# Layer 0 of a hybrid decoder step: the next step's distances issued one by one between this step's masked copies

## The chip, the core and the metric

The kernel runs on one core of a Trainium2 chip. The metric is the device time of one launch in microseconds. A core has five engines with an instruction queue each, worked off in order: TensorE (PE in the profile, its weight loads PEld), VectorE (DVE), ScalarE (ACT), GpSimd (POOL) and SyncE (SP), which issues most DMAs here. They wait for each other through semaphores: an instruction raises a counter when it is done, and another engine, or the same one, waits until the counter has reached a value.

## The reference

One inference step of a two-layer trunk, float32. Layer 0 mixes tokens by gated linear attention (GLA), layer 1 by a Mamba-2 state space scan; both have RMS norms before and after, and a gate. There are 16 meta tokens, a prompt of 1024 tokens and 8 samples of one token each. The part that the change touches is the attention inside a chunk:

```
bcum   = cumsum(log_alpha)                                   # per head channel k, falling
decay  = exp(where(i >= j, bcum[i] - bcum[j], -inf))
attn   = einsum('bihk,bjhk,bijhk->bhij', q, k, decay)
o      = attn @ v + (q * exp(bcum)) @ S
S      = exp(b_last) * S + (k * exp(b_last - bcum))^T @ v
```

The decay depends on i, j and the channel k at once, so it can't be taken out of the product as one factor.

## The kernel before

**Tiling.** All products are made in full float32 precision from pairs of rounded parts, a high one (ScalarE makes it by a copy) and a low one (VectorE subtracts the high one from the full value): high by high, high by low, low by high. The columns (8 samples, 16 meta tokens, 1024 prompt tokens) are cut into nine steps: step 0 has 24 columns, steps 1 to 8 have 128 each. They form two groups, steps 0 to 4 and 5 to 8. For each layer, group and head unit u (four units) the input projections are run tile by tile (`Pieces`), and stored in DRAM. One unit behind, the recurrent part takes the stored columns step by step. A pair (u, s) is an event e; there are 36 in each layer.

**Order.** `Plan.skeleton` writes one list of tasks, and every engine walks this list and issues its own share of each task (`program`). For layer 0 the list of a step e is `gla`; a number beside a name shifts the event, ("decay", 1) is the decay of event e+1, ("turn", -1) the turn of event e-1. "fill" puts in pieces of the projections. In this order, in the stretch that matters: distance(e+1), keys(e), levels(e), decay(e+1), turn(e-1), fill, load(e+2), fill, state(e), fill, attend(e), scale(e+1), products(e-1).

**The attention of an event.** The triangle i >= j of 128 by 128 is cut into levels: blocks of 64, 32, ..., 1, and the diagonal. In a level with blocks of h, all pairs (i, j) of a block of 2h meet at its middle, and decay = exp(bcum[i] - mid) * exp(mid - bcum[j]).
- `dve_distance` (L1707 to L1726, VectorE) writes, for each of 7 levels, bcum minus its middle into one of the eight parts of the buffer E (`g_decays`, double by e % 2): L1723. The eighth part is bcum minus its last column, for the state: L1725. This last instruction alone raises the semaphore `dsub`.
- `act_decay` (ScalarE) makes exp(bcum) (L1737), waits for `dsub`, and takes absolute value (L1739) and exp (L1741) of all eight parts at once, 128 x 1024 elements each.
- `dve_scale` (VectorE) multiplies all parts by q (L1750) and by k (L1753).
- `pe_levels` (TensorE) makes the products of each level into two banks of PSUM, L1836 and L1839, levels 0 to 3 in the first half, 4 to 6 in the second, and the plain product of q and k for the diagonal last, L1842. The semaphore `levels` rises after each half.
- `dve_levels` (VectorE) picks from each bank, through a mask, the blocks of a level, and puts them into one matrix `g_attn`: six copies L1857 (levels 0 and 1 share one), and the diagonal L1861. All write the same matrix, so each waits for the one before by the semaphore `attn_part`.
- `pe_attend` (TensorE, L1933) multiplies `g_attn` with the values, `dve_gate` (L1940) gates the result, `pe_turn` (L1959) transposes it. `act_turn` (ScalarE, L1968) copies its high part to `g_ot_hi`, `dve_turn` (VectorE, L1976) makes the low part `g_ot_lo`, and `pe_products` (TensorE, helper line L790) multiplies with the output weights; before it, TensorE waits for `g_ot_lo`.

On ScalarE a step's queue is so: keys (L1811), decay of the next event (L1737, L1739, L1741), turn of the event before (L1968), then roundings of weights (L805), of `h` (L1387), and evictions of projection pieces. On VectorE: the eight distances of e+1, keys (step 0 only), the copies of e, `g_ot_lo` of e-1, work for pieces, state (L1926), gate (L1940), scaling of e+1.

Of the kernel before, what the change touches and what calls it, by code (L numbers as in the profile page):

```python
# [9 lines left out]
ALU = mybir.AluOpType  # L10
ACT = mybir.ActivationFunctionType

P = 128
D = 1024
KT = D // P
NS = 8
# [33 lines left out]
EVENTS = [(u, s) for G in range(2) for u in range(U) for s in GROUP_STEPS[G]]  # L50
# [5 lines left out]
def step_cols(s):  # L56

    return (0, C0) if s == 0 else (C0 + P * (s - 1), P)
# [6 lines left out]
def ev(u, s):  # L65

    return 5 * u + s if s < 5 else 5 * U + 4 * u + s - 5
# [7 lines left out]
def gla_levels(s):  # L75

    return ([8, 4, 2, 1], NS) if s == 0 else ([64, 32, 16, 8, 4, 2, 1], 0)


def gla_masks(s):  # L80

    return [0, 1, 2, 3] if s == 0 else [0, 2, 3, 4, 5, 6]
# [29 lines left out]
class Plan:  # L112
# [72 lines left out]
    def skeleton(self):  # L185
# [3 lines left out]
        def stage(L, name, e, first_only=False):  # L189
            if 0 <= e < len(EVENTS):  # L190
# [12 lines left out]
                else:  # L203
                    tasks.append((name, L, u, s))

        gla = [("distance", 1), ("keys", 0), ("levels", 0), ("decay", 1), ("turn", -1), ("fill", 0.5), ("load", 2),
               ("fill", 0.5), ("samples", 0.4), ("state", 0), ("fill", 0.5), ("attend", 0), ("scale", 1),
               ("products", -1), ("weight", 0, 0), ("values", 1), ("square", 0), ("r_add", -2), ("r_in", -1),
               ("fill", 0.5), ("lows",), ("fill", 0.5), ("weight", 1, 0), ("r_square", -1), ("r_out", -2),
# [1350 lines left out]
class Gla:  # L1560
# [143 lines left out]

    def dve_distance(self, dve, u, s):  # L1707
        t, e, n = self.t, ev(u, s), step_cols(s)[1]
        if e == 0:
            dve.wait_ge(self.zeros, 4)  # L1710
            dve.wait_ge(self.consts, self.CONSTS)
        x, E = self.tokens(u, s), t["E"][:, e % 2, :, :]
        sizes, off = gla_levels(s)
        dve.wait_ge(self.ck_in[e % 2], 16 * (e // 2 + 1))
        if e >= 2:
            dve.wait_ge(self.levels, 2 * (e - 1))
            dve.wait_ge(self.tb_done, e - 1)
        b = x[:, 2, off:n]
        if s == 0:
            dve.memset(E[:, :, 0:NS], 0.0).then_inc(self.zeros, 1)  # L1720
        for li, h in enumerate(sizes):
            v = b.rearrange("p (b w) -> p b w", w=2 * h)
            dve.tensor_tensor(E[:, li, off:n].rearrange("p (b w) -> p b w", w=2 * h), v,  # L1723
                              v[:, :, h - 1:h].to_broadcast([P, v.shape[1], 2 * h]), ALU.subtract)
        dve.tensor_tensor(E[:, 7, off:n], b, x[:, 2, n - 1:n].to_broadcast([P, n - off]),  # L1725
                          ALU.subtract).then_inc(self.dsub, 1)  # L1726

    def act_decay(self, act, u, s):
        t, e, n = self.t, ev(u, s), step_cols(s)[1]
# [113 lines left out]
            last.then_inc(self.levels, 1)  # L1843

    def dve_levels(self, dve, u, s):
        t, e, n = self.t, ev(u, s), step_cols(s)[1]
        g, mk = (t["G0"], t["mask0"]) if s == 0 else (t["G"], t["mask"])
        masks = gla_masks(s)
        if e:
            dve.wait_ge(self.o_done, e)  # L1850
        part = sum(len(gla_masks(q)) for _, q in EVENTS[:e])
        for i, li in enumerate(masks):
            if li % 4 == 0:
                dve.wait_ge(self.levels, 2 * e + li // 4 + 1)
            if i:
                dve.wait_ge(self.attn_part, part + i)
            dve.copy_predicated(g[:, :], mk[:, li, :].bitcast(I32),  # L1857
                                self.L[li // 4][0:n, (li % 4) * P:(li % 4) * P + n]).then_inc(self.attn_part, 1)
        dve.wait_ge(self.attn_part, part + len(masks))
        dve.wait_ge(self.levels, 2 * e + 2)  # L1860
        dve.copy_predicated(g[:, :], self.m["ident"][0:n, 0:n].bitcast(I32),  # L1861
                            self.L[1][0:n, 3 * P:3 * P + n]).then_inc(self.attn, 1)

# [728 lines left out]
```

## Time and profile before

| | |
|---|---|
| median of 3 runs | 1641.74 us (1635.92 to 1644.21) |
| the profiled execution | 1636.64 us, its span 1634.9 us |
| TensorE busy | 1518.6 us (93%) |
| VectorE busy | 1186.8 us (73%) |
| ScalarE busy | 824.5 us (50%) |
| GpSimd busy | 238.6 us (15%) |
| masked copies L1857, 192 of 128x128 | 57.9 us, 301 ns each |
| distances L1723, 224 of 128x128 | 47.8 us, 282 ns each |
| mean granted TensorE clock | 0.972 of full |

Busy time of an engine is the union of its instructions. Idle time of an engine that is not the bottleneck costs nothing by itself; it counts where the engine that is nearly always busy waits for it. A line of the profile names the engine, the source line, the operation, and "written tile <- read tiles". The recurrent part of layer 0 runs from about 85 to 740 us of the span. In a timeline, "idle before <- releaser" stands in brackets where an engine stood idle.

### The profile page before, as it was taken

The numbers are of one execution on the slowest core, as the hardware profiler recorded it, in microseconds if no ns is written. First come the engines' busy times: TensorE is split into PE (matmuls) and PEld (weight loads), VectorE is DVE, ScalarE is ACT, GpSimd is POOL, SyncE is SP. The second block draws the span as 40 slices with busy tenths as digits, with TensorE's granted clock in tenths as the row PEclk, the third lists the DMA queues.
The fourth block names the chain that finished last, engine by engine and source line by source line (L and its number), as shares of the span: only waits on it lengthen the run. The fifth ranks groups of instructions, "written<-read, shape, count | busy, mean of one in ns | idle before, by whom it ended". The sixth has DMA issues, their size and how long they took to land. (4 is left out here: it accounts for less than half of the span.)

```text
span 1634.9 us, 26150 instructions
## 1 busy us (share of the span) xinstructions
PE 1518.6 (93%) x8970; PEld 1266.4 (77%) x8970; DVE 1186.8 (73%) x2587; ACT 824.5 (50%) x1835; POOL 238.6 (15%) x427
## 2 busy tenths in 40 slices
PE   6989999899999979898999999889989999999876
PEld 5979777667878869898888888767777778778654
DVE  4556477957786887868887798876769676587665
ACT  4634343445455545546664664544546364554441
POOL 5010112001220200112110220210002110000002
PEclk8999999999999999999999999999999999999998
DMA  6454454344565533448855765743675765556641
GB/s 172 135 156 117 133 148 144 106 138 141 150 156 174 149 114 100 130 111 204 230 141 127 228 167 129 216 121 83 190 189 139 180 166 138 163 142 158 149 142 58
DMA packets 312095, 242.60 MB, mean 148 GB/s; under 512 B 32760, under 2 KB 283452, under 8 KB 311804
## 3 DMA queue, kind: packets, MB, share of 16 engines
q1 hardware_dynamic: 302140, 208.28, 47.3%
q0 software_dynamic: 9824, 32.64, 7.3%
q8 instruction: 73, 1.20, 0.3%
q14 instruction: 58, 0.48, 0.1%
HBM read 180.40 MB, written 64.97 MB: 150 GB/s over the span
## 5 line engine op out<-in xcount | busy, mean ns | idle before, releaser
L1377 PE MATMUL bank<-h,w 128*128 128x268 f32 (+1 forms) x4752 | 840.8, 331 | 32.7 <-ACT w L805 28.0
L1377 PEld LDWEIGHTS bank<-h,w 128*128 128x128 f32 x4752 | 704.4, 192 | 110.6 <-issue 41.2
L790 PE MATMUL bank<-s_w_out,s_yt_hi 128*128 128x512 f32 (+1 forms) x576 | 186.6, 405 | 15.7 <-DVE s_w_out L821 6.9
L819 DVE TENSOR_TENSOR w<-w_raw,w 128x1024 fp32r<-128x1024 f32 x132 | 160.9, 1219 | 52.5 <-ACT w L805 52.1
L805 ACT ACTIVATE w<-w_raw 128x1024 fp32r<-128x1024 f32 x132 | 138.7, 1051 | 37.7 <-DMA w_raw<-in_ssd_w_in_dram 37.2
L790 PEld LDWEIGHTS bank<-s_w_out,s_yt_hi 128*128 128x128 f32 (+1 forms) x576 | 103.0, 183 | 46.5 <-issue 8.9
L1455 DVE SCALAR_TENSOR_TENSOR conv<-before_conv,cw,conv 128x260 f32<-128x260 f32 (+2 forms) x216 | 125.2, 580 | 4.3
L790 PE MATMUL bank<-s_w_out,s_yt_lo 128*128 128x512 f32 (+1 forms) x288 | 115.3, 400 | 0.0
L790 PE MATMUL bank<-g_w_out,g_ot_hi 128*128 128x512 f32 (+1 forms) x288 | 100.5, 431 | 0.0
L2210 ACT ACTIVATE s_decay<-s_decay,t_ac 128x128 f32<-128x128 f32 (+1 forms) x288 | 85.4, 379 | 1.2
L1857 DVE COPY_PREDICATED g_attn<-g_lmask,bank 128x128 f32<-128x128 int32 (+1 forms) x208 | 60.6, 291 | 33.8 <-PE bank L1839 25.7
L1423 ACT ACTIVATE conv<-bank,cw 128x268 f32<-128x268 f32 (+1 forms) x72 | 45.9, 637 | 74.3 <-PE bank L1377 61.5
L2384 PEld LDWEIGHTS bank<-s_xdt,s_decay 128*128 128x128 f32 (+1 forms) x576 | 66.5, 183 | 19.3 <-issue 19.3
L1699 POOL TENSOR_SCALAR g_omean<-g_osum 128x1 f32<-128x1 f32 (+1 forms) x36 | 16.5, 459 | 431.0 <-ACT squares L1951 431.0
L2185 POOL TENSOR_SCALAR s_ymean<-s_ysum 128x1 f32<-128x1 f32 (+1 forms) x36 | 18.8, 521 | 399.5 <-ACT squares L2486 399.3
L2505 ACT ACTIVATE s_yt_hi<-bank 128x512 fp32r<-128x512 f32 (+1 forms) x36 | 20.0, 556 | 112.2 <-PE bank L2496 112.1
L2168 POOL DMA_DIRECT2D out_dram<-s_sample_state x32 | 25.1, 784 | 331.2 <-DVE s_sample_state L2322 331.2
L1527 DVE SCALAR_TENSOR_TENSOR stage<-stage,conv 128x268 f32<-128x268 f32 (+1 forms) x72 | 37.3, 518 | 49.2 <-ACT stage L1484 48.7
L1789 ACT ACTIVATE g_vr_turned<-bank 128x512 f32<-128x512 f32 (+1 forms) x36 | 21.3, 591 | 91.0 <-PE bank L1777 91.0
L790 PEld LDWEIGHTS bank<-g_w_out,g_ot_hi 128*128 128x128 f32 (+1 forms) x288 | 53.5, 188 | 17.4 <-issue 2.9
L2023 DVE SCALAR_TENSOR_TENSOR y_acc<-bank,s_yrstd,y_acc 128x512 f32<-128x512 f32 (+1 forms) x54 | 39.7, 745 | 35.5 <-PE bank L790 35.5
L2384 PE MATMUL bank<-s_xdt,s_decay 128*128 128x64 f32 (+1 forms) x576 | 65.3, 266 | 0.0
(230 smaller groups left out, 2513.8 us busy)
## 6 DMA issues: line engine op xcount, KB each, us to landing
w_raw<-in_ssd_w_in_dram SPq DMA_DIRECT2D x80, 512.0 KB, 4.2
w_raw<-in_gla_w_in_dram SPq DMA_DIRECT2D x48, 512.0 KB, 4.2
s_decay<-kept_acd SPq DMA_DIRECT2D x32, 512.0 KB, 8.4
w_raw<-in_ssd_w_out_dram SPq DMA_DIRECT2D x32, 512.0 KB, 4.3
g_chunk<-kept_gq SPq DMA_DIRECT2D x32, 448.0 KB, 5.0
s_chunk<-kept_sq SPq DMA_DIRECT2D x32, 384.0 KB, 4.9
kept_sq<-stage SPq DMA_DIRECT2D x80, 134.0 KB, 4.2
kept_sq<-stage SPq DMA_DIRECT2D x40, 256.0 KB, 4.6
```

Of the source, the lines that this page charges most:

```text
L790: last = pe.matmul(bank[0:n, :], yt[a][:, k, 0:n], wo[:, k, b, 512 * half:512 * half + 512], start=(k + a + b == 0), stop=(k == tiles - 1 ...
L805: act.activation(self.part(i, 0), self.raw(i), ACT.Copy).then_inc(self.w_hi, 1)
L819: dve.tensor_tensor(self.part(i, 1), self.raw(i), hi, ALU.subtract).then_inc(self.w_lo, 1)
L1377: last = pe.matmul(bank[:, 0:n], w[:, p.tile % 2, a, k, :], h[:, b, k, c:c + n], start=(i == 0), stop=(i == len(terms) - 1))
L1423: act.activation(self.work(i)[:, 0:n], bank[:, 0:n], ACT.Identity, scale=m["cw"][:, 3, a:a + 1], bias=m["cw"][:, 4, a:a + 1])
L1455: return dve.scalar_tensor_tensor(out=u[:, off:n], in0=x[:, k:k + w], scalar=cw[:, k, a:a + 1], in1=u[:, off:n], op0=ALU.mult, op1=ALU.add)
L1527: dve.scalar_tensor_tensor(out=self.slot(i)[:, 0:n], in0=self.slot(i)[:, 0:n], scalar=1.0, in1=self.work(i)[:, 0:n], op0=ALU.add, op1=ALU. ...
L1857: dve.copy_predicated(g[:, :], mk[:, li, :].bitcast(I32), self.L[li // 4][0:n, (li % 4) * P:(li % 4) * P + n]).then_inc(self.attn_part, 1)
L2023: return dve.scalar_tensor_tensor(out=y, in0=bank, scalar=rstd, in1=y, op0=ALU.mult, op1=ALU.add)
L2168: pool.dma_start(self.heads(self.d["ssm_sample"][0, b], u), self.t["ss"][:, i % SAMPLES, :, :]).then_inc(self.ss_out[i % SAMPLES], 16)
L2210: last = act.activation(L[0:n, r, :], L[0:n, r, :], ACT.Relu, scale=-1.0, bias=ac[0:n, s, h:h + 1])
L2384: last = pe.matmul(self.Y[0][0:n, r * HD:(r + 1) * HD], G[0:n, r, :], t["xdt"][0:n, r * HD:(r + 1) * HD], start=True, stop=True)
```

## The change

The task "distance" is taken out of the list `gla`, so that in the loop over events no distances are issued ahead of the copies. (The one for event 0, in the list `start`, stays.) `dve_levels` of event e now issues the distances of event e+1 itself: what they wait for and the first one ahead of the first masked copy, then one behind each masked copy, and the rest behind the diagonal copy. In an event of 128 columns that is: distance 0, six times copy and distance, diagonal copy, distance 7, the one that raises `dsub`. In an event of 24 columns it is distance 0, four times copy and distance, diagonal copy, and the remaining three. The arithmetic, the number of instructions, the buffers and the other engines' programs are the same.

```diff
-        gla = [("distance", 1), ("keys", 0), ("levels", 0), ("decay", 1), ("turn", -1), ("fill", 0.5), ("load", 2),
+        gla = [("keys", 0), ("levels", 0), ("decay", 1), ("turn", -1), ("fill", 0.5), ("load", 2),
...
+    def distance_ready(self, dve, u, s):
+        e = ev(u, s)
         if e == 0:
             dve.wait_ge(self.zeros, 4)
             dve.wait_ge(self.consts, self.CONSTS)
...
+    def distance(self, dve, u, s, li):
+
+        t, e, n = self.t, ev(u, s), step_cols(s)[1]
+        sizes, off = gla_levels(s)
+        b, E = self.tokens(u, s)[:, 2, off:n], t["E"][:, e % 2, li, off:n]
+        if li == 7:
+            dve.tensor_tensor(E, b, b[:, n - off - 1:n - off].to_broadcast([P, n - off]),
+                              ALU.subtract).then_inc(self.dsub, 1)
+        elif li < len(sizes):
+            h = sizes[li]
+            v = b.rearrange("p (b w) -> p b w", w=2 * h)
+            dve.tensor_tensor(E.rearrange("p (b w) -> p b w", w=2 * h), v,
+                              v[:, :, h - 1:h].to_broadcast([P, v.shape[1], 2 * h]), ALU.subtract)
...
     def dve_levels(self, dve, u, s):
...
+        following = EVENTS[e + 1] if e + 1 < len(EVENTS) else None
+        if following:
+            self.distance_ready(dve, *following)
+            if following[1] == 0:
+                dve.memset(t["E"][:, (e + 1) % 2, :, 0:NS], 0.0).then_inc(self.zeros, 1)
+            self.distance(dve, *following, 0)
         if e:
             dve.wait_ge(self.o_done, e)
...
             dve.copy_predicated(g[:, :], mk[:, li, :].bitcast(I32),
                                 self.L[li // 4][0:n, (li % 4) * P:(li % 4) * P + n]).then_inc(self.attn_part, 1)
+            if following:
+                self.distance(dve, *following, i + 1)
         dve.wait_ge(self.attn_part, part + len(masks))
         dve.wait_ge(self.levels, 2 * e + 2)
         dve.copy_predicated(g[:, :], self.m["ident"][0:n, 0:n].bitcast(I32),
                             self.L[1][0:n, 3 * P:3 * P + n]).then_inc(self.attn, 1)
+        if following:
+            for li in range(len(masks) + 1, 8):
+                self.distance(dve, *following, li)
```

## Rows read from the trace of the kernel before

**Rows 1.** Busy by stretch, layer 0: PE, PEld, DVE, ACT, POOL; clock, DMA, GB/s.
```profile
85.00:740.00 655.00, 624.42 (x3829) 521.32 (x3830) 471.02 (x1105) 310.80 (x617) 95.86 (x160) 0.98 0.48 135
```

**Rows 2.** Waits, 85 to 740 us: who <- for whom: us, times, longest.
```profile
ACT g_decays L1739 <- DVE g_decays L1725: 46.6, 25, 3.7
...
DVE g_attn L1857 <- PE bank L1839: 25.7, 12, 5.6
...
PE bank L1377 <- ACT w L805: 8.9, 3, 4.7
...
PE bank L1933 <- DVE g_attn L1861: 7.1, 3, 3.9
PE bank L1016 <- DVE h L1435: 6.8, 3, 3.1
```

**Rows 3.** Timeline of VectorE, one step: start, us, engine, line, operation.
```profile
573.68 1.50 DVE L1723 TENSOR_TENSOR g_decays<-g_chunk 128x128 f32<-128x128 f32 x7
575.10 0.28 DVE L1725 TENSOR_TENSOR g_decays<-g_chunk 128x128 f32<-128x128 f32 x1
575.30 2.04 DVE L1857 COPY_PREDICATED g_attn<-g_lmask,bank 128x128 f32<-128x128 int32 x6
577.38 0.30 DVE L1861 COPY_PREDICATED g_attn<-ident,bank 128x128 f32<-128x128 int32 x1
577.87 0.42 DVE L1976 TENSOR_TENSOR g_ot_lo<-bank,g_ot_hi 128x256 fp32r<-128x256 f32 x1 [0.18 <-ACT g_ot_hi L1968]
```

**Rows 4.** Timeline of ScalarE, the same step.
```profile
575.41 1.06 ACT L1739 ACTIVATE g_decays<-g_decays 128x1024 f32<-128x1024 f32 x1 [2.54 <-DVE g_decays L1725]
576.50 1.06 ACT L1741 ACTIVATE g_decays<-g_decays 128x1024 f32<-128x1024 f32 x1
577.47 0.37 ACT L1968 ACTIVATE g_ot_hi<-bank 128x256 fp32r<-128x256 f32 x1
```

**Rows 5.** Timeline of TensorE, the same step.
```profile
577.82 0.62 PE L1933 MATMUL bank<-g_vr_turned,g_attn 128*128 128x256 f32 x2
578.35 0.73 PE L790 MATMUL bank<-g_w_out,g_ot_hi 128*128 128x512 f32 x2
```

**Rows 6.** Timeline of VectorE, a copy followed by an instruction that isn't held.
```profile
444.60 0.30 DVE L1861 COPY_PREDICATED g_attn<-ident,bank 128x128 f32<-128x128 int32 x1
444.81 0.42 DVE L1976 TENSOR_TENSOR g_ot_lo<-bank,g_ot_hi 128x256 fp32r<-128x256 f32 x1
```

**Rows 7.** Timeline of VectorE, four other steps.
```profile
298.93 1.48 DVE L1723 TENSOR_TENSOR g_decays<-g_chunk 128x128 f32<-128x128 f32 x7
...
303.11 0.42 DVE L1976 TENSOR_TENSOR g_ot_lo<-bank,g_ot_hi 128x256 fp32r<-128x256 f32 x1 [0.19 <-ACT g_ot_hi L1968]
...
460.29 0.42 DVE L1976 TENSOR_TENSOR g_ot_lo<-bank,g_ot_hi 128x256 fp32r<-128x256 f32 x1 [0.19 <-ACT g_ot_hi L1968]
...
565.82 0.42 DVE L1976 TENSOR_TENSOR g_ot_lo<-bank,g_ot_hi 128x256 fp32r<-128x256 f32 x1 [0.19 <-ACT g_ot_hi L1968]
...
591.07 0.42 DVE L1976 TENSOR_TENSOR g_ot_lo<-bank,g_ot_hi 128x256 fp32r<-128x256 f32 x1 [0.20 <-ACT g_ot_hi L1968]
```

**Rows 8.** Timeline of TensorE, these four steps and one wait for weights.
```profile
300.61 0.39 PE L1842 MATMUL bank<-g_chunk 128*128 128x128 f32 x2
...
303.58 0.72 PE L790 MATMUL bank<-g_w_out,g_ot_hi 128*128 128x512 f32 x2
...
463.84 0.81 PE L790 MATMUL bank<-g_w_out,g_ot_hi 128*128 128x512 f32 x2
...
566.99 0.81 PE L790 MATMUL bank<-g_w_out,g_ot_hi 128*128 128x512 f32 x2
...
591.59 1.42 PE L790 MATMUL bank<-g_w_out,g_ot_hi 128*128 128x512 f32 x2
...
675.70 4.36 PE L1377 MATMUL bank<-h,w 128*128 128x268 f32 x18 [4.70 <-ACT w L805]
```

**Rows 9.** Timeline of ScalarE, the rounding of weights behind that wait.
```profile
674.51 1.05 ACT L805 ACTIVATE w<-w_raw 128x1024 fp32r<-128x1024 f32 x1
```

## What the change should do to the time

> **What bounds the kernel now.** I read the busy times first, of the stretch that the edit touches (layer 0, 85 to 740 us of the span): of its 655 us TensorE is busy for 624.4, VectorE for 471.0, ScalarE for 310.8 [rows 1]. A change on VectorE can only show where TensorE stands still, 30.6 us now, or will. Next came the waits of that window [rows 2]. TensorE waits there for the last masked copy (L1933, 7.1 us in 3 waits), for the `h` tile that a norm piece needs (L1016, 6.8 us in 3) and for weights rounded by ScalarE (L1377, 8.9 us in 3). The longest wait that the change is bound to touch is on neither engine: ScalarE waits 46.6 us, in 25 of 36 steps, for the last distance, before the absolute value in `act_decay` (L1739). And VectorE waits 25.7 us, in 12 steps, for the level products on TensorE (L1857). These 12 are steps in which VectorE comes early; in the others it comes late, with everything else ready.
>
> Then one late step in order of time, engine by engine [rows 3 to 5]. VectorE does seven distances from 573.68, the last (L1725) until 575.38, six masked copies from 575.30, the diagonal copy until 577.68, then waits 0.18 us for `g_ot_hi` and splits off `g_ot_lo` until 578.29. ScalarE starts Abs at 575.41, 0.03 us after the last distance, Exp at 576.50 and the copy to `g_ot_hi` at 577.47, one right behind the other. TensorE starts `attend` (L1933) at 577.82 and the output products (L790) at 578.35, 0.06 us after `g_ot_lo`. So two chains end at about the same point of TensorE's queue: copies -> attend, and last distance -> Abs -> Exp -> `g_ot_hi` -> `g_ot_lo` -> products. The second is 0.5 us the later one, and it is the one that hangs on the distances.
>
> **The change, part by part.** No instruction and no DMA goes or comes; what moves is the order on VectorE. In a full step (128 columns, followed by another such) there are 8 distances and 7 copies.
>
> Spacing. Distances start 0.20 us apart ((575.30-573.68)/8), though each is 0.28 long: they overlap. Copies that wait for one another start 0.347 apart ((577.38-575.30)/6) [rows 3]. An instruction that isn't held starts 0.20 us after a copy has started: 444.60 to 444.81 [rows 6]. So I take copy, distance 0.20 later, next copy 0.20 after that, at 0.404, when its predecessor's signal (0.347) is already there. From the start of the step: 0.20 for distance 0, six pairs of 0.404, diagonal copy from 2.63 to 2.93, last distance from 2.83 to 3.11. Before: diagonal copy ended at 4.00, last distance at 1.70. Hence the attention matrix is ready 1.07 us earlier, VectorE is through 0.89 us earlier, and the last distance comes 1.41 us later.
> Bounds for the last distance: if the distances vanish wholly behind the held copies (pair 0.347), it ends at 2.76, +1.06. If nothing overlaps (pair 0.347+0.202), at 3.97, +2.27, with attention only 0.2 earlier. No bound reaches zero, because the last distance stands behind six chained copies in any case. I take +1.41, since rows 6 show the overlap directly.
> The Trainium skill ("VectorE: DVE Perf Modes", section "The DRAIN you can't avoid") says that a signal between chained operations costs nothing and that the flush is paid either way. By it the upper bound would hold: +2.27, and some 31 us in all. The 0.347 against 0.20 above speaks against it here.
>
> Abs, Exp and `g_ot_hi` stand in ScalarE's queue in this order, before and after, and all pass the +1.41 on: in rows 4 there is no idle time between them. Behind `g_ot_lo` in VectorE's queue are the state update, the gate and the next scaling, so VectorE as well comes out 1.4 us later; the 0.89 us that it saved is spent idle, waiting for `g_ot_hi`. Ahead of the products in TensorE's queue stands only `attend`, which may start up to 1.07 us earlier but gains nothing, the products behind it being late. Cost of a step = delay of `g_ot_lo` minus its slack before the products:
> - No slack: four steps, at 216.7, 480.2, 578.35 and 591.59 us; the last two stand in rows 5, 7 and 8. The gap from the end of `g_ot_lo` (591.49) to the products is 0.1. 1.35 to 1.44 each, 5.5 us. The three waits on the last copy in rows 2 are among them: they get shorter, and the wait for the products takes their place.
> - Partial slack: five steps (products at 231.8, 245.2, 293.1, 540.8, 567.0). The last: `g_ot_lo` ends at 566.24, products 566.99, slack 0.75, delay 1.8, since the copies there also wait a little for the levels; loss 1.08. The five: 0.86, 0.89, 1.09, 1.12, 1.08, together 5.0 us. Two more lose 0.3 together.
> - One step with the levels barely late: VectorE starts at 298.93, the levels end at 300.61+0.39=301.00. Copies could start before only because distances filled the time; now the first must wait for the first half of the levels (about 0.9 us before their end, an estimate from L1842's place in rows 8), and the last distance ends at 303.07 in place of 300.61, +2.46. `g_ot_lo` ended at 303.53, products 303.58 [rows 7, 8]: 2.4 us.
> - The same ScalarE delay by another road, three places. At 675.70 TensorE has waited 4.70 us for weights whose rounding (L805) started at 674.51, straight behind `g_ot_hi` in ScalarE's queue [rows 8, 9]. In two others (L1016, rows 2; at 315.6 and 604.8) it waits for `h`, whose ScalarE half stands behind `g_ot_hi` too. 1.4 each, 4.2 us.
> - The other 16 steps of 128 columns: nothing. Where the levels are late, Abs used to run under that wait and now starts after the last copy, so `g_ot_hi` is up to 3.7 us late; the slack there is larger. The nearest is the step at 460: `g_ot_lo` ended at 460.71, products 463.84, slack 3.13 against a delay of 2.74 [rows 7, 8]. What hides them is the projection matmuls between levels and `attend`. If that cover were 0.5 us thinner, some four of these steps would cost a few tenths each, 2 us.
> Sum: 5.5+5.0+0.3+2.4+4.2 = 17.4 us.
> Clock. After the 3.9 us wait in front of L1933 two output products took 1.42 us (591.59), against 0.73 at 578.35 [rows 5, 8]: the array ran at the lower of its two levels, 1.2 GHz, there. Longer stalls will bring one or two more such stretches; a stretch that covers two such pairs and what lies between costs about 1.5 us, and I add it once: 18.9 us.
> The four steps of 24 columns have four short copies, and TensorE's sample work stands between them and the products; they count as zero.
> The profiled execution took 1636.64 us with a span of 1634.9: 1636.6+18.9 = 1655.5. The median of the runs is 1641.74, 5.1 above it; from there it would be 1660.6. I say 1657.
>
> **Rivals.**
> *Covered.* Some stalls are given back later: TensorE comes later, so DMA and norm waits in front of it shrink, and the 15 places don't add up. For: seven of the fifteen cost 1.1 us or less each and hang on slacks of tenths. Against: the chain in rows 3 to 5 has idle time nowhere. With more than half given back, +5 to +8: 1642 to 1649.
> *Faster.* VectorE is the bound in the stretch from 573.68 to 591.41, where it pauses only for 0.2 us at a time, and TensorE stands still there for the last copy. If attention is what decides, each of the three waits of L1933 gets up to 1.07 shorter (2.6 us), and the three behind `h` and weights 0.89 (2.7 us): 1636.6-5.3 = 1631, or 1636 from the median. It decides only if `g_ot_hi` comes no later than before, that is, if ScalarE had over 1.4 us of room before Abs; the 0.03 us in rows 4 says it has none.
> *No overlap.* Copies and distances cost what they cost apart; +2.27 per step. About 0.86 more at 14 places, 12 us, plus steps whose slack falls: 1668 to 1672. The change would then not do what its order is meant for, hiding the signal of one copy behind a distance. Against: rows 6.
>
> **How the numbers follow.** Forecast (1649 to 1664) 0.64; covered 0.16; faster 0.08; no overlap 0.12. Range 1645 to 1668: down into the covered case, up to the low end of no overlap. 0.5% of the median is 8.2 us, which is what a measurement can tell here: slower 0.78 (forecast, no overlap and the upper edge of covered), same 0.14, faster 0.08.
>
> **What would show it.** In the changed kernel, the wait of Abs for the last distance should grow from 46.6 us in 25 to 100 us or more, in over 30 steps. The wait of `g_ot_lo` for `g_ot_hi` should grow from 0.2 us to over 2 us in a full late step (VectorE through at 3.1, `g_ot_lo` at 5.6 us). TensorE's wait for the last copy (L1933) should all but go, and one in front of L790 for `g_ot_lo`, absent now, should come with 8 to 14 us. A pair of copy and distance should take 0.40 us, and a full step 3.1 us from first distance to last. TensorE's idle time from 85 us to the end of layer 0, 30.6 us now, should be near 48, and that stretch about 19 us longer. I am wrong if L790 does not wait, or if the distances and copies take 4 us as before.

## The result: 34 us slower, nearly twice the forecast

| | before | after |
|---|---|---|
| median | 1639.4 us (4 runs, 1635.9 to 1644.2) | 1673.5 us (4 runs, 1672.7 to 1677.9) |
| span of the profiled execution | 1634.9 us | 1672.5 us |
| ratio | | 1.0216, 95% interval 1.0192 to 1.0240 |

The change makes the kernel 2.2% slower. The forecast was 1657 us, 1645 to 1668: the direction and the main mechanism came as said, the size did not.

The page after, its head and the busy time of TensorE and VectorE. The instruction count is the same; VectorE is 19.5 us less busy than before, and the kernel is longer.
```profile
span 1672.5 us, 26150 instructions
PE 1533.9 (92%) x8970; PEld 1274.2 (76%) x8970; DVE 1167.3 (70%) x2587; ACT 824.9 (49%) x1835; POOL 237.3 (14%) x427
```
Layer 0 as one window, to answer [rows 1]. It ends 36.5 us later, so the window goes to 776.5. TensorE's idle time in it is 691.5-639.7 = 51.8 us, against 30.6. The mean granted clock fell from 0.98 to 0.96.
```profile
85.00:776.50 691.50, 639.67 (x3830) 529.73 (x3829) 451.50 (x1108) 311.01 (x617) 94.50 (x160) 0.96 0.45 128
```
The waits of this window, to answer [rows 2] (L1749 is the Abs that was L1739, L1998 `g_ot_lo`, L1955 `attend`, L1905 the product with a sample state).
```profile
ACT g_decays L1749 <- DVE g_decays L1723: 129.1, 34, 5.1
...
DVE g_ot_lo L1998 <- ACT g_ot_hi L1990: 79.7, 34, 2.5
...
DVE g_attn L1874 <- PE bank L1849: 39.0, 14, 7.5
...
PE bank L790 <- DVE g_ot_lo L1998: 13.4, 10, 2.4
...
PE bank L1016 <- DVE h L1435: 10.4, 3, 4.6
...
PE bank L1377 <- ACT w L805: 9.9, 4, 4.4
...
PE bank L1905 <- DMA g_sample_state<-in_state_gla_dram: 4.8, 3, 2.6
...
PE bank L1955 <- DVE g_attn L1880: 4.5, 2, 2.8
```
The wait of Abs went from 46.6 us in 25 steps to 129.1 in 34. A wait for `g_ot_lo` in front of the output products is new, 13.4 us in 10. The waits of L1016 and L1377 grew by 3.6 and 1.0. The one for the last copy (L1955) shrank by 2.6 but did not go. The one for the DMA of a sample state (L1905, L1883 before) grew by 2.8; before it was
```profile
PE bank L1883 <- DMA g_sample_state<-in_state_gla_dram: 2.0, 2, 1.6
```

The same step as in [rows 3 to 5], VectorE first.
```profile
601.46 0.28 DVE L1728 TENSOR_TENSOR g_decays<-g_chunk 128x128 f32<-128x128 f32 x1
601.67 0.29 DVE L1874 COPY_PREDICATED g_attn<-g_lmask,bank 128x128 f32<-128x128 int32 x1
601.86 0.28 DVE L1728 TENSOR_TENSOR g_decays<-g_chunk 128x128 f32<-128x128 f32 x1
602.07 0.29 DVE L1874 COPY_PREDICATED g_attn<-g_lmask,bank 128x128 f32<-128x128 int32 x1
...
604.07 0.29 DVE L1880 COPY_PREDICATED g_attn<-ident,bank 128x128 f32<-128x128 int32 x1
604.27 0.28 DVE L1723 TENSOR_TENSOR g_decays<-g_chunk 128x128 f32<-128x128 f32 x1
607.03 0.43 DVE L1998 TENSOR_TENSOR g_ot_lo<-bank,g_ot_hi 128x256 fp32r<-128x256 f32 x1 [2.49 <-ACT g_ot_hi L1990]
```
ScalarE and TensorE in it.
```profile
604.58 1.06 ACT L1749 ACTIVATE g_decays<-g_decays 128x1024 f32<-128x1024 f32 x1 [4.59 <-DVE g_decays L1723]
605.67 1.06 ACT L1751 ACTIVATE g_decays<-g_decays 128x1024 f32<-128x1024 f32 x1
606.64 0.37 ACT L1990 ACTIVATE g_ot_hi<-bank 128x256 fp32r<-128x256 f32 x1
```
```profile
605.69 0.59 PE L1955 MATMUL bank<-g_vr_turned,g_attn 128*128 128x256 f32 x2
607.51 0.72 PE L790 MATMUL bank<-g_w_out,g_ot_hi 128*128 128x512 f32 x2 [1.23 <-DVE g_ot_lo L1998]
```
A pair of distance and copy takes 0.40 us. From the step's start the last distance ends at 3.09 (forecast 3.11) and the diagonal copy at 2.90 (2.93). VectorE then stands idle for 2.49 us, until ScalarE is through Abs, Exp and `g_ot_hi`; TensorE stands idle behind it.

What the forecast did not have is in the step of 24 columns at 182 us, where samples are updated. Before and after on VectorE (`g_ot_lo` and the first updates of a sample state, L1901, now L1923).
```profile
184.35 0.41 DVE L1976 TENSOR_TENSOR g_ot_lo<-bank,g_ot_hi 128x256 fp32r<-128x256 f32 x1
186.40 0.87 DVE L1901 SCALAR_TENSOR_TENSOR g_sample_state<-g_sample_state,g_ebcum,bank 128x256 f32<-128x256 f32 x2 [1.64 <-PE bank L1891]
```
```profile
188.27 0.42 DVE L1998 TENSOR_TENSOR g_ot_lo<-bank,g_ot_hi 128x256 fp32r<-128x256 f32 x1 [2.49 <-ACT g_ot_hi L1990]
188.61 0.86 DVE L1923 SCALAR_TENSOR_TENSOR g_sample_state<-g_sample_state,g_ebcum,bank 128x256 f32<-128x256 f32 x2
```
GpSimd's issue of the load of a later sample state, before and after. It stands behind the store of the updated state in GpSimd's queue. A load runs three samples ahead, so this one brings the state of the step's fourth sample.
```profile
188.36 0.73 POOL L1676 DMA_DIRECT2D g_sample_state<-in_state_gla_dram  x1
```
```profile
190.56 0.73 POOL L1676 DMA_DIRECT2D g_sample_state<-in_state_gla_dram  x1
```
TensorE, at that fourth sample, before and after.
```profile
193.68 1.04 PE L1883 MATMUL bank<-g_sample_state,g_q_masked 128*24 128x256 f32 x4 [0.46 <-DMA g_sample_state<-in_state_gla_dram]
194.65 1.13 PE L1891 MATMUL bank<-g_vr_turned,g_k_masked 24*128 24x256 f32 x4
195.71 1.00 PE L1377 MATMUL bank<-h,w 128*128 128x268 f32 x6
```
```profile
196.06 1.12 PE L1905 MATMUL bank<-g_sample_state,g_q_masked 128*24 128x256 f32 x4 [2.62 <-DMA g_sample_state<-in_state_gla_dram]
197.11 2.07 PE L1913 MATMUL bank<-g_vr_turned,g_k_masked 24*128 24x256 f32 x4
199.11 1.71 PE L1377 MATMUL bank<-h,w 128*128 128x268 f32 x6
```
The wait is 2.2 us longer, and the same six projection matmuls take 1.71 us in place of 1.00. The windows say why, before and after (last but two columns: granted clock): 1.2 GHz, the lower level, for nearly the whole stretch.
```profile
193.00:205.00 12.00, 11.54 (x66) 8.67 (x66) 4.97 (x10) 3.85 (x8) 3.32 (x6) 1.00 0.44 147
```
```profile
196.90:210.60 13.70, 13.70 (x38) 9.44 (x37) 4.13 (x7) 1.25 (x2) 2.17 (x3) 0.50 0.24 83
```
Between the level products of this step (ended 182.5, now 182.7) and of the next (207.65+0.39 = 208.0, now 216.20+0.39 = 216.6) 8.3 us were lost, of which 2.2 are idle time.

### The profile page after: what moved, and what is told of

Same layout as the page of the kernel before. It is cut to its first block, busy times and chain, and to the rows that moved or that the text cites. A ratio compares the mean times of both kernels' runs of the same rounds, so it can differ in the third digit from the quotient of the medians.

```text
span 1672.5 us, 26150 instructions
## 1 busy us (share of the span) xinstructions
PE 1533.9 (92%) x8970; PEld 1274.2 (76%) x8970; DVE 1167.3 (70%) x2587; ACT 824.9 (49%) x1835; POOL 237.3 (14%) x427
## 4 chain that ended last, share of the span: by engine, by line
PE 35%; DVE 5%; DMA 5%; ACT 3%; issue 2%; SPq 1%; POOL 0%; ACTq 0%; DVEq 0%; POOLq 0%
PE bank L1377 15%; PE bank L790 12%; DMA w_raw<-in_ssd_w_out_dram 2%; PE bank L2406 2%; DMA w_raw<-in_ssd_w_in_dram 1%; PE bank L2398 1%; PE bank L2401 1%; DMA kept_sq<-stage 1%; DVE s_w_out L821 1%; DVE w L819 1%; PE bank L2485 1%; PE bank L2518 1%; ACT s_decay L2232 1%; PE bank L2258 1%; PE bank L2320 1%
## 5 line engine op out<-in xcount | busy, mean ns | idle before, releaser
L1377 PE MATMUL bank<-h,w 128*128 128x268 f32 (+1 forms) x4752 | 841.6, 331 | 35.1 <-ACT w L805 29.4
L1377 PEld LDWEIGHTS bank<-h,w 128*128 128x128 f32 x4752 | 704.7, 192 | 115.0 <-issue 43.8
L790 PE MATMUL bank<-s_w_out,s_yt_hi 128*128 128x512 f32 (+1 forms) x576 | 189.3, 411 | 15.6 <-DVE s_w_out L821 6.8
L790 PEld LDWEIGHTS bank<-s_w_out,s_yt_hi 128*128 128x128 f32 (+1 forms) x576 | 104.5, 186 | 47.4 <-issue 8.9
L790 PE MATMUL bank<-s_w_out,s_yt_lo 128*128 128x512 f32 (+1 forms) x288 | 116.8, 405 | 0.0
L790 PE MATMUL bank<-g_w_out,g_ot_hi 128*128 128x512 f32 (+1 forms) x288 | 104.2, 446 | 13.4 <-DVE g_ot_lo L1998 13.4
L1749 ACT ACTIVATE g_decays<-g_decays 128x1024 f32<-128x1024 f32 (+1 forms) x36 | 35.3, 981 | 129.1 <-DVE g_decays L1723 129.1
L790 PEld LDWEIGHTS bank<-g_w_out,g_ot_hi 128*128 128x128 f32 (+1 forms) x288 | 55.5, 197 | 34.4 <-DVE g_ot_lo L1998 17.4
L1998 DVE TENSOR_TENSOR g_ot_lo<-bank,g_ot_hi 128x256 fp32r<-128x256 f32 (+1 forms) x36 | 14.4, 400 | 79.7 <-ACT g_ot_hi L1990 79.7
L2045 DVE SCALAR_TENSOR_TENSOR y_acc<-bank,s_yrstd,y_acc 128x512 f32<-128x512 f32 (+1 forms) x54 | 39.9, 745 | 37.8 <-PE bank L790 37.8
```

Source lines behind the costliest of these rows:

```text
L790: last = pe.matmul(bank[0:n, :], yt[a][:, k, 0:n], wo[:, k, b, 512 * half:512 * half + 512], start=(k + a + b == 0), stop=(k == tiles - 1 ...
L1377: last = pe.matmul(bank[:, 0:n], w[:, p.tile % 2, a, k, :], h[:, b, k, c:c + n], start=(i == 0), stop=(i == len(terms) - 1))
L1749: act.activation(E, E, ACT.Abs).then_inc(self.dabs, 1)
L2045: return dve.scalar_tensor_tensor(out=y, in0=bank, scalar=rstd, in1=y, op0=ALU.mult, op1=ALU.add)
```

## Experiments

Ratios are to the kernel before, which was measured again beside each group of experiments, with their 95% interval.

**1. The delay of Abs alone.** VectorE's order is the old one; ScalarE waits longer.
```diff
         act.wait_ge(self.dsub, e + 1)
+        if e:
+            act.wait_ge(self.attn_part, sum(len(gla_masks(q)) for _, q in EVENTS[:e]) - 2)
         act.activation(E, E, ACT.Abs).then_inc(self.dabs, 1)
```


> The kernel before with one more wait: Abs of event e+1 on ScalarE also waits for the last but one masked copy of event e. VectorE's order stays that of before, so its last distance ends 1.70 us into a full step, but Abs can start only about 3.0 us into it (1.62 + 3 x 0.347 + 0.30), 1.3 to 1.4 us later, as in the changed kernel. Theory A (the loss comes through Abs, Exp and g_ot_hi alone): 1665 to 1680 us, near the changed kernel's 1673, with g_ot_lo waiting about 1 us for g_ot_hi and TensorE waiting for g_ot_lo in front of the output products. Theory B (it is the order of the 15 instructions on VectorE, or copies that start later): 1637 to 1645, as before.

Measured: 1664.2 us, ratio 1.0144 (1.0126 to 1.0161), just under the expected span. Without any change on VectorE, one wait on ScalarE costs 25 of the 34 us. The wait is for the fourth of the six masked copies, not for the last but one. Its delay of Abs is the same as that of the change in a step where VectorE is late: in the one at 591.19 Abs starts 3.08 us into the step, against 3.12 above. Where the copies wait for the level products, it is smaller. One such step, the end of the level products and Abs, first here, then in the changed kernel:
```profile
247.35 0.39 PE L1844 MATMUL bank<-g_chunk 128*128 128x128 f32 x2
248.43 1.06 ACT L1741 ACTIVATE g_decays<-g_decays 128x1024 f32<-128x1024 f32 x1 [2.16 <-DVE g_attn L1859]
...
251.05 0.39 PE L1852 MATMUL bank<-g_chunk 128*128 128x128 f32 x2
253.58 1.06 ACT L1749 ACTIVATE g_decays<-g_decays 128x1024 f32<-128x1024 f32 x1 [3.61 <-DVE g_decays L1723]
```
Abs starts 0.69 us behind the products here and 2.14 there. The waits of its layer 0:
```profile
ACT g_decays L1741 <- DVE g_attn L1859: 105.5, 34, 5.1
...
DVE g_ot_lo L1978 <- ACT g_ot_hi L1970: 49.5, 31, 3.5
...
PE bank L790 <- DVE g_ot_lo L1978: 7.3, 8, 1.3
```
So the delay of Abs is sufficient for most of the loss; theory B falls. That the other 9 us come from the smaller delay was not tested by itself.

**2. The same change, with `g_ot_hi` ahead of Abs in ScalarE's queue.**
```diff
-("levels", 0), ("decay", 1), ("turn", -1), ("fill", 0.5), ("load", 2),
+("levels", 0), ("turn", -1), ("decay", 1), ("fill", 0.5), ("load", 2),
```


> The changed kernel, but ScalarE copies g_ot_hi of event e-1 ahead of Exp, Abs and the wait for the distances of event e+1, in place of behind them. VectorE's order is that of the change. Theory A: with the late distances off the way to the output products, the wait of TensorE for g_ot_lo goes and only the gains are left (attention matrix 1.07 us earlier, VectorE through 0.9 us earlier): 1630 to 1642 us. Theory B (copies or the late start of the next scaling hurt): still over 1655.

Measured: 1643.1 us, ratio 1.0019 (1.0002 to 1.0036). 30 of the 34 us are back, but the time is not below 1642 as I thought. TensorE's wait for `g_ot_lo` is gone from the list; the late Abs now shows further on. At 308.46 TensorE waits 2.05 us for the scaled decays of the next event, which it did not before, and right behind that for the accumulation (L2045), a wait that was 1.16 us at this place before. Behind the two waits the clock was lower: the ten passes of L1849 took 2.50 us, against 1.38 before.
```profile
308.46 0.30 PE L1815 MATMUL bank<-ident,g_decays 128*128 128x128 f32 x1 [2.05 <-DVE g_decays L1763]
309.98 0.70 PE L1846 MATMUL bank<-g_q_decayed,g_decays 128*64 128x64 f32 x6 [1.22 <-DVE y_acc L2045]
310.61 2.50 PE L1849 MATMUL bank<-g_q_decayed,g_decays 128*128 128x128 f32 x10
```

**3. Steps of 24 columns back in the old order.**
```diff
+                    elif name == "ahead":
+                        if s == 0:
+                            stage(L, "distance", e + 1)
...
+        following = EVENTS[e + 1] if e + 1 < len(EVENTS) and s else None
```
("ahead", 1) stands first in the list of a step.

> The changed kernel, but in the four steps of 24 columns the distances stay ahead of keys and copies, as before the change. In the trace of the changed kernel the stretch between the level products of events 5 and 6 took 8.3 us more, with one wait for a sample state's DMA of 2.6 us in place of 0.5 and 13.7 us at the lower clock. Theory A (late distances in the 24-column step delay the sample updates on VectorE, so the DMA behind them): that stretch is back within 1 us of before and the time is 1662 to 1667 us. Rival: the long low-clock stretch is chance of the profiled execution and the time stays at 1671 to 1675.

Measured: 1663.4 us, ratio 1.0143 (1.0124 to 1.0162). Of its layer 0, 682.1 us long, TensorE was busy for 632.4:
```profile
85.00:767.10 682.10, 632.40 (x3833) 524.17 (x3834) 453.55 (x1111) 310.65 (x617) 95.76 (x160) 0.97 0.46 130
```

**4. The reverse, only those steps in the new order** (the two conditions of experiment 3 turned round).

> The reverse: the distances move between the copies in the four steps of 24 columns only; all others as before. Theory A: 1645 to 1651 us, 8 to 9 above before. Rival (chance, or the full steps make it): 1637 to 1641.

Measured: 1648.2 us, ratio 1.0048 (1.0030 to 1.0066), so 9 us from the four small steps. Experiments 3 and 4 add up: 24.4+9.2 = 33.6, against 34.1 for the whole. In its profile the stretch behind 183 us lost 8.3 us again, with the same wait of 2.61 us, so it was no chance, and nearly all of the 9 us lie in this one of the four steps.

**5. Fill that wait with matmuls over 24 rows.** Based on experiment 4.
```diff
+        if (u, i) == (1, 3):
+            for _ in range(5):
+                pe.matmul(self.TA[:, HV:2 * HV], t["km"][:, 0, :], self.values(u, 0), start=True, stop=True)
         i += 4 * u
         pe.wait_ge(self.ss_in[i % SAMPLES], 16 * (i // SAMPLES + 1))
```


> The kernel with the change in the 24-column steps only (1648.2 us), and five extra matmuls of 24x256 into an unused half of a bank, in the second head unit, where TensorE stands 2.6 us for a sample state's DMA; their result is used by nobody. At full clock a pair of such matmul passes takes about 0.5 us, so they fill 2.4 us of the wait and add none. Theory A (of the 8.3 us that this stretch lost, 2.2 are idle time and 6 the lower clock that TensorE fell to behind it): the clock stays up, the stretch loses 2 to 3 us, the kernel takes 1641 to 1644. Rival (the slow matmuls there have another cause, such as contention with the sample DMAs): 1647 to 1650.

Measured: 1652.8 us, ratio 1.0070 (1.0041 to 1.0100), eight runs from 1642.9 to 1658.0; not faster than experiment 4. The profiled execution is the fastest of the eight, 10 us below the median. In it the idle time was filled, and the clock fell all the same:
```profile
192.72 2.42 PE L1906 MATMUL bank<-g_vr_turned,g_k_masked 24*128 24x256 f32 x10
195.54 1.51 PE L1911 MATMUL bank<-g_sample_state,g_q_masked 128*24 128x256 f32 x4 [0.40 <-DMA g_sample_state<-in_state_gla_dram]
196.98 2.07 PE L1919 MATMUL bank<-g_vr_turned,g_k_masked 24*128 24x256 f32 x4
```
The stretch lost 8.4 us. My reading that the idle time itself had dropped the clock failed here.

**6. Fill it with matmuls over 128 rows.** The same, with `pe.matmul(self.TA[:, HV:2 * HV], self.S[:, 0, 0:P], self.S[:, 0, :], ...)`, the finished state of head unit 0 as weights and data. Two things differ from experiment 5: the rows in use, 128 in place of 24, and the values, for all but one of the 24 rows of the masked keys are zero.

> The same five extra matmuls in the same wait, but with a full 128x128 weight tile and real data in place of 24 rows. With the 24-row ones the idle time there fell to 0.4 us and the clock fell behind it all the same, for 13.7 us. Theory C (24-row matmuls do not hold the clock, work over all rows does): clock at its upper level from 196 to 210 us, the stretch between the products of events 5 and 6 loses 2 to 3 us against before, the kernel takes 1641 to 1644. Rival D (the clock there does not depend on what fills the wait): 13.7 us at the lower level again, 1647 to 1655.

Measured: 1643.8 us, ratio 1.0030 (1.0007 to 1.0053), ten runs from 1637.1 to 1651.1. In the profile, again of the fastest run, the clock stayed up: the four matmuls of L1919 took 1.12 us in place of 2.07, and the stretch lost 2.1 us in place of 8.3.
```profile
193.78 2.32 PE L1906 MATMUL bank<-states 128*128 128x256 f32 x10
196.52 1.04 PE L1911 MATMUL bank<-g_sample_state,g_q_masked 128*24 128x256 f32 x4 [0.42 <-DMA g_sample_state<-in_state_gla_dram]
197.49 1.12 PE L1919 MATMUL bank<-g_vr_turned,g_k_masked 24*128 24x256 f32 x4
```
The interval overlaps that of experiment 4, so it is the trace of one execution that tells them apart, not the time. It puts 6.2 us of the 8.3 down to the clock.

**7 and 8. Other delays.** `double`: distances 0 and 1 ahead of the first copy, two more behind each of the first three copies. `copies_first`: all copies, then all distances.
```diff
             self.distance(dve, *following, 0)
+            self.distance(dve, *following, 1)
...
-            if following:
-                self.distance(dve, *following, i + 1)
+            if following and i < 3:
+                self.distance(dve, *following, 2 * i + 2)
+                self.distance(dve, *following, 2 * i + 3)
```


> Two distances ahead of the first copy and two behind each of the first three, the last three copies and the diagonal alone. The last distance ends at 2.3 us into a full step, 0.6 later than before the change, against 1.41 with it. Theory A: the loss shrinks with the delay, 1648 to 1658 us, the more as fewer waits drop the clock. Rival: the loss comes from interleaving as such and stays at 1665 or more.

Measured: 1659.2 us, ratio 1.0129 (1.0115 to 1.0143), a little over the span of theory A and under the rival's.

> All seven copies of event e first, then all eight distances of event e+1, in one row: the last distance ends 2.37 + 0.30 + 1.7, some 4.0 us into a full step, 2.3 later than before the change and 0.9 later than with it; attention is ready 1.6 us earlier than before. Theory A (Abs and what follows it): slower than the changed kernel, 1685 to 1700 us, in spite of the early copies. Rival (copies delayed by the distances between them are the loss): faster than the changed kernel, below 1660.

Measured: 1707.9 us, ratio 1.0422 (1.0396 to 1.0448); the rival, that the copies' delay is the loss, has the wrong sign. TensorE waits 29.4 us in 19 steps for `g_ot_lo`:
```profile
ACT g_decays L1749 <- DVE g_decays L1723: 160.1, 35, 6.0
...
PE bank L790 <- DVE g_ot_lo L1995: 29.4, 19, 3.8
```
The loss rises with the delay of the last distance in a full step (in the traces 0.6, 1.4 and 2.3 us): 21, 34 and 70 us. It isn't proportional to it. All three kernels have the long wait for a sample state; if the small steps take 9 us in each (an estimate from experiment 4), the full steps take 12, 25 and 61, so the last part of the delay is the dearest. That fits with more steps running out of slack: `g_ot_lo` holds up the products in 5, 10 and 19 steps. I had 1685 to 1700 for the last, too little again: 70 us, where 47 to 62 were expected.

**9. The swap on ScalarE alone, on the kernel before.** The diff is that of experiment 2.

> The kernel before, with the swap on ScalarE alone: g_ot_hi ahead of Abs and Exp. VectorE no longer waits 0.2 us for g_ot_hi in 18 steps, and the products can start 0.2 to 0.6 us earlier in the four steps without slack, but only behind the last copy. Theory A: 1635 to 1641 us, no change or up to 2 us faster; so the swap of ScalarE's order gives back only what the late distances took and is no gain of 30 us by itself.

Measured: 1632.9 us, ratio 0.9968 (0.9955 to 0.9980), faster than both kernels and a little beyond what I expected. The part of the swap that is a gain by itself is 5 us; of the 30 us in experiment 2, then, some 25 are what the late distances had taken by way of `g_ot_hi`. Behind the swap the new order still costs 10 us (1643.1 against 1632.9): in the two profiles layer 0 is 10.6 us longer, with 7.3 us more idle time of TensorE. Theory B of experiment 2, late scaling, fits this rest, and the wait of 2.05 us above is a piece of it; the other pieces were not followed.

**10. Swap and half the delay.** Experiments 7 and 2 together.

> Two distances behind each of the first three copies, and ScalarE copies g_ot_hi ahead of Abs and Exp. The last distance is 0.6 us late, off the way to the products, and attention 0.45 us early. By theory A between the kernel before with the swap (1633) and the changed kernel with the swap (1643): 1633 to 1640 us. If interleaving itself pays once g_ot_hi is out of its way, it is faster than 1633, and then late distances cost nothing any more.

Measured: 1638.1 us, ratio 0.9983 (0.9965 to 1.0001), between the two as theory A has it. No interleaving that I tried beats the plain swap.

## Why the prediction was right and wrong

- **Spacing on VectorE: right.** 0.40 us a pair, last distance at 3.09 us, attention at 2.90. The rival without overlap is out. The Trainium skill ("VectorE: DVE Perf Modes", "The DRAIN you can't avoid") says that a semaphore between chained Vector operations costs nothing extra, and also that an operation which isn't held starts earlier. The prediction's upper bound used the first and left out the second. The trace agrees with the second: 0.20 us from a copy to an operation that waits for nothing, 0.347 from a copy to the next that waits for it, and 0.40 for a copy and a distance now. What part of the 0.347 is the signal is not shown, as no run chains the copies without it.
- **The way through Abs, Exp, `g_ot_hi`: right,** by experiments 1 and 2 and the other delays of 7 and 8. The growth of the waits was forecast as 8 to 14 us for L790 (13.4), over 100 for Abs (129.1), over 2 for `g_ot_lo` in a full step (2.49). The ten steps in which TensorE now waits for `g_ot_lo` are the ten that the forecast gave a cost of their own.
- **Idle time of the full steps: right.** "Sum: 17.4 us". Experiment 3, which has the change in these steps alone, shows 682.1-632.4 = 49.7 us idle in place of 30.6: 19.1 more. The kernel took 1663.4 us there, inside the range of the forecast.
- **"They count as zero": wrong.** The four steps of 24 columns cost 9 us (experiment 4), 8.3 of them in one step. I looked at the slack of the products and found sample work in between, but did not look at what is queued on VectorE behind the waiting `g_ot_lo`: the updates of the sample states, on which GpSimd's store and, behind it in the same queue, the load of a later state hang. This is the step of the forecast that failed; without its 9 us the result would lie in the range.
- **"I add it once: 18.9 us": the clock term was mis-sized.** TensorE's idle time in layer 0 grew by 21.2 us, the layer by 36.5. The other 15 us are slower matmuls: by the mean clock of the two windows (0.98 and 0.96, so about 26 and 55 us at the lower level) roughly 29 us more at 1.2 GHz. 6 of the 15 lie in the stretch of experiment 6, the others, some 9, are spread: in experiment 3 the layer is 27.1 us longer with 19.1 more idle, so 8.0 are slower matmuls. I put 1.5 us for them. Put together, the forecast for the layer was 17.4 idle, 1.5 clock and nothing for the small steps; the profiles have 19.1, 8.0 and the rest of the 36.5, 9.4.
- **"TensorE's wait for the last copy should all but go": wrong in size.** It went from 7.1 to 4.5 us. Of the 3.9 us wait, attention could take off only its own 1.07; the rest stayed, and the wait for the products came on top.
- **"Covered": not seen.** Layer 1 kept its length within some 1 us of before (894.9 and 896.0), and TensorE's idle time in layer 0 grew by more than the sum of the places, not by less.

## What to carry to other kernels

Before moving work within one engine's queue, list every instruction that waits for the last piece of it, and what is queued behind each waiting instruction on its engine: here a semaphore raised once, by the eighth of eight distances, held 0.37 us of unrelated work behind 2.1 us of Abs and Exp. Here the stall that was saved, on an engine that isn't the bottleneck, brought nothing, and 1.4 us more on a chain that had 0.1 us of slack in a few steps and little more than its delay in others cost some 25 of the 34 us. Price an idle microsecond of TensorE at more than one: in this case 1.7 over layer 0 (1.4 in experiment 3), for the clock that falls behind it. And try the cheap reordering on the consumer's side, which here gained 5 us with no new instruction.

## What was not expected of the hardware

The granted clock fell to its lower level not only behind idle time. In experiment 5 TensorE was busy for 2.42 us with passes over 24 rows, nearly all of them zero, and idle for 0.40, and then the clock stood at its lower level for over 13 us (0.50 from 196.1 to 209.5). With passes over 128 rows of real data in the same place and 0.42 us idle (experiment 6) it stayed at 2.4 GHz (1.00 from 196 to 210). Whether the rows or the values make the difference was not tested. A reader who sees the engine busy in the trace can't conclude that the clock holds. Each is one profiled execution, and the times of both kernels scatter (15 and 14 us). The kernel before scatters as widely, 1634.4 to 1649.5 us in 23 runs. The scatter of experiment 5 goes with the clock: its three fastest runs (1642.9 to 1644.3 us) had a mean granted clock of 0.974 to 0.976, the five others (1650.2 to 1658.0) 0.963 to 0.971. In experiment 6 the two slowest (1650.5 and 1651.1) had 0.968 and 0.969, the fastest 0.976. In which stretches the clock fell in the slower ones is not shown, since only the fastest were profiled.
